# A conditioned decoder step: the two MLP products by blocks with seven half-size products each

## The chip, the core and the metric

The kernel runs on one core of a Trainium2 chip. Its engines work side by side and are tied by semaphores: TensorE (PE; its weight loads are shown as PEld), VectorE (DVE), ScalarE (ACT), GpSimd (POOL), and SyncE (SP), which here only issues DMAs. The metric is the device time of one execution in microseconds (us); lower is better.

## The reference

```python
mod = silu(c) @ w_ada + b_ada            # six vectors: sh1, sc1, g1, sh2, sc2, g2
h = rmsnorm(x, norm1_g) * (1 + sc1) + sh1
y = mixer(h, ...)                        # pooling, short convolution and Conformer heads; w_in before, w_out behind
x = x + g1 * y
h = rmsnorm(x, norm2_g) * (1 + sc2) + sh2
x = x + g2 * (square(relu(h @ w_ff1)) @ w_ff2)
out = rmsnorm(x, final_g)
```

There are 1024 prompt tokens, which share one c, and 8 sample tokens with a c each, so N = 1032 columns; the model is 1024 wide, the MLP 4096. All is float32.

## The kernel before

Activations lie transposed, features on the 128 partitions and tokens along the row: xT is 8 blocks of 128 x 1032. Every large product is made in three parts: both operands are split into a high part (float32r, a rounded copy) and a low part (the rest), and the product is high·high + high·low + low·high. `product` does this for one output block: for each block of the contraction and each of the three parts, three matmuls of TW = 344 columns.

Weights arrive by DMA in `wraw` (two slots), ACT copies them rounded to `whi` (`high`, L534), POOL subtracts to give `wlo` (`low`, L459).

The mixer ends with w_out in two parts, `p1` (contraction blocks 0 to 4) and `p2` (5 to 7), eight output blocks each; after each of them DVE adds gate times product to xT (`residual`, L951, L953, L955).

The second norm stands between `p2` and the MLP. ACT squares the rows of xT (L563), DVE adds them (`add_squares`, L963), PE sums over the partitions (`token_sums`, L1269), DVE and ACT make the factor 1/rms per token, PE spreads it (`spread`, L1298), then DVE and ACT write hhi and hlo (`h_pre` L817, `h_high` L570, `h_low` L824); POOL does the sample columns (`sample_h`, L475 to L479). `keep_clock` (L1279) gives PE matmuls of no use in between, some of 512, 258, 172 and 128 columns.

The MLP runs in groups of FG = 4 hidden blocks, in a loop that works ahead by one group. `up` makes four hidden blocks (8 x 9 matmuls each), `hidden` squares the rectified result (ACT L670, DVE L1110), and splits it (ACT L673, DVE L1114). `down` makes the share of these four blocks in all eight output blocks (4 x 9 matmuls each) and `residual` adds it to xT. Two sets of three PSUM banks alternate. The last group's `down` is done in three token tiles (`part`), so that the last norm and the output (`tile_sums`, `rows_out`) follow tile by tile.

Of the kernel before, what the change touches and what calls it, by code (L numbers as in the profile page):

```python
# [5 lines left out]
F32 = mybir.dt.float32  # L6
# [22 lines left out]
NG = FF_C // FG  # L29
# [3 lines left out]
ADA_SLOTS = 5  # L33
# [6 lines left out]
def plan():  # L40
# [42 lines left out]
    chunk("norm2", "-")  # L83
# [24 lines left out]
WARM = ((512,) * 5, (512,) * 2 + (258,) * 10 + (512,) * 2, (512,) * 4 + (172,) * 8 + (128,) * 8 + (512,) * 8)  # L108
LAG = 2
SQ = {2: 0, 3: CONV_C, 4: CONV_C + KD}  # L110
ADDED = {2: 0, 3: 1, 4: KD - 1}


def decoder_trunk(nc, x_prompt, x_sample, c_prompt, c_sample, state_pool, state_sconv, state_conf,
# [11 lines left out]
    with ctx:  # L126

        xT = sb("xT", [P, KD, N])
        whi = sb("whi", [P, 2, 8, P], F32R)
        wlo = sb("wlo", [P, 2, 8, P], F32R)  # L130
        wraw = sb("wraw", [P, 2, 8 * P])
        work = [sb(f"work{i}", [P, PAD + N]) for i in range(3)]
# [19 lines left out]
        last_cols = sb("last_cols", [P, 2, P])  # L152
        states_out = sb("states_out", [P, 2, P])
# [32 lines left out]
        hid_hi = sb("hid_hi", [P, 2 * FG, N], F32R)
        hid_lo = sb("hid_lo", [P, 2 * FG, N], F32R)

        acc = ctx.enter_context(nc.psum_tensor("acc", [P, 2, 3, 512], F32))
        modps = ctx.enter_context(nc.psum_tensor("modps", [P, 512], F32))  # L190
        tps = ctx.enter_context(nc.psum_tensor("tps", [P, 512], F32))
# [1417 lines left out]
```

## Time and profile before

| | |
|---|---|
| median of 3 runs (lowest to highest) | 1138.33 us (1138.1 to 1138.94) |
| the profiled execution | 1138.9 us, span 1136.8 us |
| mean granted clock of TensorE | 0.983 |
| PE, DVE, ACT, POOL busy | 97%, 47%, 22%, 22% |
| DMA | 83.15 MB, mean 73 GB/s |

The span runs from the first to the last instruction of the core; the rest of the execution's time lies around it. Busy time counts an engine's instructions with a waiting time for operands or ports in them; a busy PE is one whose matmuls follow each other.

### The profile page before, as it was taken

To read this page: it belongs to the slowest core of one execution; us is meant where nothing else is said; L and a number is where in the kernel's file an instruction comes from. 1 tells how busy PE (TensorE), PEld (TensorE's weight loads), DVE (VectorE), ACT (ScalarE), POOL (GpSimd) and SP (SyncE) were. 2 spreads that over 40 slices of the span, in tenths; PEclk is the share of its full clock that TensorE was granted. 3 is DMA by queue.
4 is the path that set the end of the run, shared out by engine and by line. 5 is a ranking of instruction groups with operands and counts; after the bars stand their busy time and mean duration, and the time that the engine had idled before them with its cause. 6 is when DMAs were issued, how large, how long until landed. Compare 5 with 4: busy or idle time off the path is not lost.

```text
span 1136.8 us, 16478 instructions
## 1 busy us (share of the span) xinstructions
PE 1108.3 (97%) x7060; PEld 1078.0 (95%) x7060; DVE 531.0 (47%) x670; ACT 244.6 (22%) x269; POOL 255.5 (22%) x190
## 2 busy tenths in 40 slices
PE   7899999999999999999999999999999999999996
PEld 5688889999999899999999999999999999999996
DVE  4899999996367731222132223122222222312355
ACT  6321121112234332211210311220221130122111
POOL 2732122221112121212121212121212121213200
PEclk8899999999899899999999999999999999999999
DMA  9988211201111011111111111111111111111212
GB/s 282 319 294 304 66 38 38 56 24 47 29 56 56 19 48 46 55 39 54 40 52 42 44 50 43 51 41 54 38 56 38 55 39 55 39 55 41 72 51 99
DMA packets 97172, 83.15 MB, mean 73 GB/s; under 512 B 2663, under 2 KB 92718, under 8 KB 95039
## 3 DMA queue, kind: packets, MB, share of 16 engines
q1 hardware_dynamic: 96350, 80.87, 23.0%
q8 instruction: 59, 0.97, 0.3%
q0 software_dynamic: 336, 0.58, 0.2%
q10 hardware_dynamic: 417, 0.65, 0.2%
q14 instruction: 10, 0.08, 0.0%
HBM read 77.77 MB, written 4.81 MB: 73 GB/s over the span
## 4 chain that ended last, share of the span: by engine, by line
PE 88%; DVE 7%; SPq 2%; issue 1%; DMA 1%; POOL 0%; ACT 0%; DVEq 0%; POOLq 0%
PE acc L1237 76%; PE acc L1258 4%; DVE dc L895 4%; SPq L346 1%; PE acc L1528 1%; PE acc L1526 1%; PE acc L1527 1%; PE tps L1269 1%; DMA ada<-in_w_ada 1%; PE modps L1371 1%; DVE work L914 1%; PE acc L1555 1%; PE modps L1349 1%; DVE work L1178 1%; PE modps L1279 1%
## 5 line engine op out<-in xcount | busy, mean ns | idle before, releaser
L459 POOL TENSOR_TENSOR wlo<-wraw,whi 128x1024 fp32r<-128x1024 f32 (+2 forms) x89 | 210.2, 2362 | 785.3 <-ACT whi L534 785.3
L534 ACT ACTIVATE whi<-wraw 128x1024 fp32r<-128x1024 f32 (+2 forms) x89 | 90.9, 1022 | 684.4 <-PE acc L1237 644.7
L1237 PE MATMUL acc<-hhi,whi 128*128 128x344 f32 x1080 | 230.4, 322 | 2.1 <-issue 1.5
L1237 PE MATMUL acc<-hlo,whi 128*128 128x344 f32 x1080 | 229.0, 320 | 0.0
L1237 PE MATMUL acc<-hhi,wlo 128*128 128x344 f32 x1080 | 228.1, 320 | 0.0
L1237 PEld LDWEIGHTS acc<-hhi,whi 128*128 128x128 f32 x1080 | 181.4, 188 | 6.7 <-issue 6.5
L1237 PEld LDWEIGHTS acc<-hlo,whi 128*128 128x128 f32 x1080 | 182.6, 189 | 0.0
L1237 PEld LDWEIGHTS acc<-hhi,wlo 128*128 128x128 f32 x1080 | 180.1, 188 | 0.0
L951 DVE SCALAR_TENSOR_TENSOR xT<-acc,modT,xT 128x688 f32<-128x688 f32 x72 | 67.2, 934 | 236.7 <-PE acc L1237 235.9
L1110 DVE SCALAR_TENSOR_TENSOR work<-acc,work 128x1032 f32<-128x1032 f32 x32 | 39.4, 1232 | 249.7 <-ACT work L670 249.7
L1237 PE MATMUL acc<-hid_hi,whi 128*128 128x344 f32 x672 | 142.2, 320 | 0.0
L1237 PE MATMUL acc<-hid_lo,whi 128*128 128x344 f32 x672 | 142.0, 320 | 0.0
L1237 PE MATMUL acc<-hid_hi,wlo 128*128 128x344 f32 x672 | 142.0, 320 | 0.0
L895 DVE SCALAR_TENSOR_TENSOR dc<-glu,tapT,dc 128x1023 f32<-128x1023 f32 (+14 forms) x90 | 136.3, 1515 | 2.9
L1237 PEld LDWEIGHTS acc<-hid_lo,whi 128*128 128x128 f32 x672 | 113.0, 188 | 0.0
L1237 PEld LDWEIGHTS acc<-hid_hi,whi 128*128 128x128 f32 x672 | 112.6, 188 | 0.0
L1237 PEld LDWEIGHTS acc<-hid_hi,wlo 128*128 128x128 f32 x672 | 112.4, 188 | 0.0
L1114 DVE TENSOR_TENSOR hid_lo<-work,hid_hi 128x1032 fp32r<-128x1032 f32 x32 | 39.5, 1233 | 39.1 <-ACT hid_hi L673 39.1
L673 ACT ACTIVATE hid_hi<-work 128x1032 fp32r<-128x1032 f32 x32 | 34.1, 1067 | 42.1 <-DVE work L1110 42.1
L953 DVE SCALAR_TENSOR_TENSOR xT<-acc,modT,xT 128x336 f32<-128x336 f32 x72 | 40.2, 558 | 0.0
L670 ACT ACTIVATE work<-acc 128x1032 f32<-128x1032 f32 x32 | 32.5, 1015 | 0.0
L1526 PE MATMUL acc<-hid_hi,hhi 128*128 128x344 f32 x96 | 31.2, 325 | 0.0
(181 smaller groups left out, 981.3 us busy)
## 6 DMA issues: line engine op xcount, KB each, us to landing
wraw<-in_w_ff SPq DMA_DIRECT2D x64, 512.0 KB, 3.8
ada<-in_w_ada SPq DMA_DIRECT2D x16, 1024.0 KB, 8.4
wraw<-in_w_in SPq DMA_DIRECT2D x17, 512.0 KB, 4.7
ada<-in_w_ada SPq DMA_DIRECT2D x16, 512.0 KB, 7.4
xrow<-in_x_prompt SPq DMA_DIRECT2D x8, 512.0 KB, 9.0
out<-work SPq DMA_DIRECT2D x6, 512.0 KB
wraw<-in_w_out SPq DMA_DIRECT2D x8, 320.0 KB, 3.2
wraw<-in_w_out SPq DMA_DIRECT2D x4, 384.0 KB, 3.1
```

The source lines that it names most:

```text
L459: nc.gpsimd.tensor_tensor(o, a, b, ALU.subtract).then_inc(wlo_ready, 1)
L534: nc.scalar.activation(whi[:, slot, 0:n, :].rearrange("p k n -> p (k n)"), wraw[:, slot, 0:n * P], ACT.Copy).then_inc(whi_ready, 1)
L670: nc.scalar.activation(tiled(wk[0]), flat(acc[:, (C_FF + j) % 2, :, :]), ACT.Relu).then_inc(relu_ready, 1)
L673: nc.scalar.activation(hid_hi[:, slot + j, :], wk[1 + j % 2][:], ACT.Copy).then_inc(hid_hi_ready, 1)
L895: ins = nc.vector.scalar_tensor_tensor(dc[:, c, s:T], glu[:, c, 0:T - s], tapT[:, tap:tap + 1], dc[:, c, s:T], ALU.mult, ALU.add)
L951: nc.vector.scalar_tensor_tensor(pair(xT[:, d, 0:2 * TW]), ps[:, 0:2, 0:TW], g1, pair(xT[:, d, 0:2 * TW]), ALU.mult, ALU.add)
L953: nc.vector.scalar_tensor_tensor(xT[:, d, 2 * TW:T], ps[:, 2, 0:w2], g1, xT[:, d, 2 * TW:T], ALU.mult, ALU.add)
L1110: nc.vector.scalar_tensor_tensor(tiled(q), flat(acc[:, (C_FF + j) % 2, :, :]), 0.0, tiled(wk[0]), ALU.max, ALU.mult).then_inc(freed_v, 1)
L1114: nc.vector.tensor_tensor(hid_lo[:, slot + j, :], q[:], hid_hi[:, slot + j, :].bitcast(F32), ALU.subtract).then_inc(hid_lo_ready, 1)
L1237: last = nc.tensor.matmul(out[:, t, 0:TW], w[:, slot, b, :], x[:, k, t * TW:(t + 1) * TW], start=(i == 0 and w is whi and x is hi), stop=( ...
L1258: last = nc.tensor.matmul(outs[j][:, t, 0:TW], w[:, (u0 + j) % 2, k, :], x[:, k, t * TW:(t + 1) * TW], start=(k == 0 and w is whi and x is ...
L1526: nc.tensor.matmul(bank[:, 0:TW], w_hi, hi[:, k, cols], start=(b == 0), stop=False)
```

## The change

Both MLP products are made by blocks of 2 x 2 with seven half-size products in place of eight (Strassen's scheme in Winograd's form).

*Up.* A unit is 256 hidden features (two blocks m). The contraction is cut in pairs of blocks (KP = 4), the tokens in two halves of 524 columns (two tiles of HT = 262: 256 tokens, columns for the shift and for the samples). POOL makes the weight sums (`mix_weights`), ACT and POOL split the seven weights in four groups (`high_split`, `low_split`), each with one buffer; the operand sums are made once (`mix_rows`, `mix`, `oper_high`, `oper_low`). PE makes product p as 4 x 3 x 2 matmuls. Products share banks X, Y and V and go on accumulating in them: p0, p2, p4, p6 in X, p1 in Y, p3, p5 in V. After p0, p2 and p3 ACT copies the bank to a tile C (`copy_c`), DVE adds the bank after p1, p4 and p5 (`add_c`), and takes p6 as it is (`last_c`).

*Second norm.* The products are made from x times gain, without the factor of the token; the factor `rb` is multiplied in behind them (`scale_c`), the shift rides along as a column (`shift_c`). The sums for it are made during unit 1. norm2's stage and `keep_clock` are gone.

*Between.* `activate` (ACT) makes relu and square of each quarter C, DVE its four sums (`mix_hidden`), and SP stores seven tiles of 128 x 524 a unit in DRAM (`hid_home`; four tiles for the last two units, without sums). xT's storage is used for the tiles C, so x is stored in DRAM as well (`x_home`) and returns late (`return_x`, `rejoin`).

*Down.* Seven groups of four hidden blocks; a group has four pairs of output blocks (m = 0 to 27), product p of a pair is 2 x 3 x 2 matmuls of QT = 258 columns, and DVE gathers each bank into y (`gather`). Two weight units to a group. The activations return through twelve stages (`load_queue`) and are split again (`queue_high` on ACT, `queue_low` on DVE). The eighth group is plain, in four token quarters (`part`, 384 matmuls).

*Other.* Four slots for w_ada instead of five; the samples' row comes out as a ninth block; all loops are written out.

```diff
-ADA_SLOTS = 5
+ADA_SLOTS = 4
+HT = 262
+QT = 258
+NP = 7
+KP = 4
+UP = FF_C // 2
+GROUPS = 7
+PAIRS = 4
+FIRST_OF_CHAIN = (0, 1, 3)
+GROUP_ENDS = (1, 3, 5, 6)
...
+            def mix_weights(unit):
+                pool.wait_ge(raw_loaded[unit % 2], raw_at(unit))
+                if unit:
+                    pool.wait_ge(split_lo, 4 * unit)
...
+                link(nc.gpsimd.tensor_tensor(s3, a21, a11, ALU.subtract))
+                link(nc.gpsimd.tensor_tensor(a21, a21, a22, ALU.add))
+                link(nc.gpsimd.tensor_tensor(s2, a21, a11, ALU.subtract))
+                nc.gpsimd.tensor_tensor(s4, a12, s2, ALU.subtract).then_inc(mixed_ready, 1)
...
+            for unit in range(1, UP + 2 * GROUPS):
+                mix_weights(unit)
+                for g in range(4):
+                    low_split(unit, g)
...
+            def high_split(unit, g):
+                act.wait_ge(raw_loaded[unit % 2], raw_at(unit))
...
+                    act.wait_ge(product_made, spent(unit - 1, g))
+                if g:
+                    act.wait_ge(mixed_ready, unit + 1)
...
+            def activate(unit, n):
+                act.wait_ge(c_scaled, 4 * unit + n + 1)
+                tile = halves(c_tile(unit, n))
+                nc.scalar.activation(tile[:, :, 0:QT], tile[:, :, 0:QT], ACT.Relu, bias=tile[:, 0, 260:261]
+                                     ).then_inc(rect_ready, 1)
+                act.wait_ge(rect_ready, 4 * unit + n + 1)
+                nc.scalar.activation(tile[:, :, 0:QT], tile[:, :, 0:QT], ACT.Square).then_inc(hid_ready, 1)
...
+            for unit in range(2, UP):
+                copy_c(unit, 0, BANK_X[unit % 2], 0)
...
+                high_split(unit + 1, 0)
+                activate(unit, 0)
...
+                copy_c(unit, 2, BANK_X[unit % 2], 2)
...
+                copy_c(unit, 1, BANK_V, 3)
+                high_split(unit + 1, 1)
...
+                activate(unit, 1)
...
+                high_split(unit + 1, 2)
+                activate(unit, 2)
...
+                high_split(unit + 1, 3)
+                activate(unit, 3)
...
+            def mix_hidden(unit):
+                dve.wait_ge(hid_ready, 4 * unit + 4)
+                c11, c22, c21, c12 = [c_tile(unit, c) for c in range(4)]
+                nc.vector.tensor_tensor(c12, c12, c11, ALU.subtract).then_inc(t_ready, 1)
...
+                nc.vector.tensor_tensor(t_tile(2), c22, c12, ALU.subtract).then_inc(t_ready, 1)
+                dve.wait_ge(t_ready, 4 * unit + 2)
+                nc.vector.tensor_tensor(t_tile(3), c11, t_tile(2), ALU.subtract).then_inc(t_ready, 1)
+                nc.vector.tensor_tensor(t_tile(5), c21, t_tile(2), ALU.subtract).then_inc(t_ready, 1)
...
+            for unit in range(2, UP):
+                if unit < UP - 1:
+                    mix_hidden(unit - 1)
+                add_c(unit, 0, BANK_Y, 1, 1)
+                scale_c(unit, 0)
...
+                add_c(unit, 1, BANK_X[unit % 2], 4, 2)
+                scale_c(unit, 1)
...
+                add_c(unit, 2, BANK_V, 5, 3)
+                scale_c(unit, 2)
...
+                last_c(unit)
...
+                for j in range(PAIRS):
...
+                    gather(m + j, 0, g == 0)
+                    gather(m + j, 1, g == 0)
+                    if j < 3:
+                        queue_low(n + 3 * j)
+                    elif not last:
+                        queue_low(n + 8)
+                    gather(m + j, 2, g == 0)
...
+            def product_of(p, bank, blocks, tiles, pieces, width):
+                for n, i in enumerate(blocks):
+                    for w, x in ((0, 0), (0, 1), (1, 0)):
+                        for t in tiles:
+                            last = nc.tensor.matmul(banks[:, bank + t, 0:width], weight(p, w, i),
+                                                    operand(p, x, pieces[n], t, width),
...
+                product_of(0, x, every, both, every, HT).then_inc(product_made, 1)
...
+                product_of(1, BANK_Y, every, both, every, HT).then_inc(product_made, 1)
+                pe.wait_ge(copied, ahead + 1)
+                pe.wait_ge(split_lo, split_at(unit, 1))
+                product_of(2, x, every, both, every, HT).then_inc(product_made, 1)
...
+                product_of(3, BANK_V, every, both, every, HT).then_inc(product_made, 1)
...
+                pe.wait_ge(copied, ahead + 2)
+                pe.wait_ge(split_lo, split_at(unit, 2))
+                product_of(4, x, every, both, every, HT).then_inc(product_made, 1)
```

In the down loop (not shown) p2 of a pair waits for gather 0, p4 for gather 2, p5 for gather 3, p6 for gather 4; in the queue of DVE the fourth pair of a group has six queue_low, after gathers 1, 2, 4, 5 and twice after 6, the first two pairs three (after 1, 5, 6), the third two.

## Rows read from the trace of the kernel before

**Rows 1.** The page, part 1: busy us, share of the span, instructions.

```profile
PE 1108.3 (97%) x7060; PEld 1078.0 (95%) x7060; DVE 531.0 (47%) x670; ACT 244.6 (22%) x269; POOL 255.5 (22%) x190
```

**Rows 2.** The page, part 4: the chain that ended last, by engine.

```profile
PE 88%; DVE 7%; SPq 2%; issue 1%; DMA 1%; POOL 0%; ACT 0%; DVEq 0%; POOLq 0%
```

**Rows 3.** Windows by stage: length, busy of each engine (instructions), clock, DMA share, GB/s.

```profile
331.60:365.80 34.20, 34.13 (x217) 33.87 (x216) 21.77 (x33) 11.03 (x11) 7.95 (x4) 1.00 0.21 61
365.80:385.60 19.80, 18.28 (x87) 15.71 (x87) 11.90 (x19) 7.47 (x10) 7.55 (x6) 0.74 0.09 26
...
408.60:748.00 339.40, 338.66 (x2148) 338.38 (x2148) 88.14 (x115) 67.73 (x67) 72.17 (x30) 1.00 0.16 49
748.00:1066.00 318.00, 317.20 (x2013) 316.92 (x2012) 84.86 (x125) 58.60 (x57) 74.38 (x31) 1.00 0.17 50
1066.00:1136.80 70.80, 61.26 (x415) 59.42 (x413) 37.65 (x78) 11.98 (x27) 0.00 (x0) 0.97 0.16 61
```

**Rows 4.** PE, 172 columns: timeline (start, us to the last end), then group (mean ns).

```profile
381.03 1.04 PE L1279 MATMUL modps<-yc_hi 128*128 128x172 f32 x8
...
L1279 PE MATMUL modps<-yc_hi 128*128 128x172 f32 x8 | 1.0, 271 | 0.0
```

**Rows 5.** DVE's groups by shape: count, busy us, mean ns, idle before.

```profile
L951 DVE SCALAR_TENSOR_TENSOR xT<-acc,modT,xT 128x688 f32<-128x688 f32 x72 | 67.2, 934 | 236.7 <-PE acc L1237 235.9
L953 DVE SCALAR_TENSOR_TENSOR xT<-acc,modT,xT 128x336 f32<-128x336 f32 x72 | 40.2, 558 | 0.0
L1114 DVE TENSOR_TENSOR hid_lo<-work,hid_hi 128x1032 fp32r<-128x1032 f32 x32 | 39.5, 1233 | 39.1 <-ACT hid_hi L673 39.1
L1110 DVE SCALAR_TENSOR_TENSOR work<-acc,work 128x1032 f32<-128x1032 f32 x32 | 39.4, 1232 | 249.7 <-ACT work L670 249.7
...
L1161 DVE TENSOR_TENSOR work<-work 128x344 f32<-128x344 f32 x18 | 9.2, 514 | 7.2 <-ACT work L720 7.2
```

**Rows 6.** The same of POOL and of ACT.

```profile
L459 POOL TENSOR_TENSOR wlo<-wraw,whi 128x1024 fp32r<-128x1024 f32 x77 | 190.3, 2471 | 699.0 <-ACT whi L534 699.0
L459 POOL TENSOR_TENSOR wlo<-wraw,whi 128x640 fp32r<-128x640 f32 x8 | 12.5, 1564 | 62.1 <-ACT whi L534 62.1
...
L534 ACT ACTIVATE whi<-wraw 128x1024 fp32r<-128x1024 f32 x77 | 81.6, 1060 | 621.0 <-PE acc L1237 581.3 <-DMA wraw<-in_w_in 34.1 <-PE acc L1258 5.6
...
L554 ACT ACTIVATE work<-acc 128x344 f32<-128x344 f32 x6 | 2.7, 457 | 5.9 <-PE acc L1298 5.6
```

**Rows 7.** Two lines' durations (min/median/max ns), then timelines of DVE and POOL.

```profile
L967 DVE TENSOR_TENSOR small<-gate_s,modT x9: 224/2095/2133, 333.2 to 1070.5; 128x64 f32<-128x64 f32 x9
...
L1110 DVE SCALAR_TENSOR_TENSOR work<-acc,work x32: 1232/1232/1234, 406.5 to 1025.8; 128x1032 f32<-128x1032 f32 x32
...
358.44 2.40 POOL L459 TENSOR_TENSOR wlo<-wraw,whi 128x1024 fp32r<-128x1024 f32 x1 [6.90 <-ACT whi L534]
...
359.85 2.07 DVE L963 TENSOR_TENSOR work<-work 128x1024 f32<-128x1024 f32 x1 [1.13 <-ACT work L563]
...
366.97 2.37 POOL L459 TENSOR_TENSOR wlo<-wraw,whi 128x1024 fp32r<-128x1024 f32 x1 [6.13 <-ACT whi L534]
...
367.29 2.13 DVE L967 TENSOR_TENSOR small<-gate_s,modT 128x64 f32<-128x64 f32 x1
...
380.05 2.70 DVE L817 SCALAR_TENSOR_TENSOR work<-xT,A,work 128x1024 f32<-128x1024 f32 x2 [4.50 <-ACT work L554]
...
380.50 1.17 POOL L476 TENSOR_TENSOR hs<-hs,A 128x64 f32<-128x64 f32 x1
```

**Rows 8.** DMA issues of w_ada: count, KB each, median us to landing.

```profile
ada<-in_w_ada SPq DMA_DIRECT2D x16, 1024.0 KB, 8.4
```

**Rows 9.** PE in the norm: timeline, then windows with the granted clock.

```profile
366.70 1.03 PE L1269 MATMUL tps<-ones,work 128*128 128x1 f32 x8
...
368.00:370.00 2.00, 2.00 (x9) 0.51 0.00 0
370.00:378.00 8.00, 8.00 (x32) 0.50 0.23 66
```

More of the change, by code:

```diff
@@ new lines, in stage_loads, with queue_free, stored_tiles, stored_at @@
+def stage_loads(n):
+    return 16 * sum(stage_of(m) == stage_of(n) for m in range(n + 1))
+def queue_free(n):
+    g, p, _ = QUEUE[n]
+    if g == GROUPS:
+        return made(UP + PAIRS * (GROUPS - 2) + PAIRS - 1, 3 + p)
+    if g == 0 or (g == 1 and p >= 3):
+        return made(UP - 1, p)
+    return made(UP + PAIRS * (g - (2 if p >= 3 else 1)) + PAIRS - 1, p)
+def stored_tiles(unit):
+    return NP if unit < UP - 2 else 4
+def stored_at(unit):
+    return 16 * sum(stored_tiles(v) for v in range(unit % 2, unit + 1, 2))
@@ L186, in decoder_trunk @@
[L186 to L191, printed above, removed]
+        xrow = span(H_AT, KD * D).rearrange("p (i n) -> p i n", n=D)
+        rest = H_AT + KD * D
+        xsrow = span(rest, D)[0:S]
+        crow = span(rest + D, D)[0:32]
@@ new lines, in _, with queue_low @@
+            diagonals(3, diag2)
+            add_c(1, 0, BANK_Y, 1, 1)
+            dve.wait_ge(rb_ready, 3)
+            dve.wait_ge(copied, 4)
+            scale_c(0, 0)
+            scale_c(0, 1)
+            scale_c(0, 2)
+            scale_c(0, 3)
+            scale_c(1, 0)
+            add_c(1, 1, BANK_X[1], 4, 2)
+            scale_c(1, 1)
+            add_c(1, 2, BANK_V, 5, 3)
+            scale_c(1, 2)
+            mix_hidden(0)
+            last_c(1)
+            def queue_low(n):
+                dve.wait_ge(queue_hi, n + 1)
+                nc.vector.tensor_tensor(queue_piece(n, 1), stage(n), queue_piece(n, 0).bitcast(F32), ALU.subtract
+                                        ).then_inc(queue_lo, 1)
@@ L1532, in tile_sums, with operand @@
-            def tile_sums(t):
-                pe.wait_ge(ms_ready, 3 + t)
-                for d in (0, KD - 1):
-                    if d:
-                        pe.wait_ge(sq_ready, SQ[4] + t * KD + KD)
-                    else:
-                        pe.wait_ge(sq_added, ADDED[4] + (t + 1) * (KD - 2))
-                    for q in range(3):
-                        last = nc.tensor.matmul(tps[:, 3 * t + q:3 * t + q + 1], sq_part(d)[:, SUB[q]:SUB[q] + P],
-                                                ones[:, 0:1], start=(d == 0 and q == 0), stop=(d > 0),
-                                                skip_group_check=True)
+            def operand(p, h, i, t, width):
+                return halves(piece(i, h, p))[:, t, 0:width]
@@ new lines, in up @@
+            def up(p, bank, blocks, tiles):
+                for i in blocks:
+                    pe.wait_ge(oper_lo, LO_AT[i, p])
+                    last = product_of(p, bank, [i], tiles, [i], HT)
+                return last
+            every = range(KP)
+            both = (0, 1)
+            x0, x1 = BANK_X
+            freed(CHUNK_AT[("p2", KD - 2)])
+            pe.wait_ge(ext_ready, 1)
+            pe.wait_ge(split_lo, split_at(0, 0))
+            up(0, x0, (0, 1), (0,))
+            pe.wait_ge(split_lo, split_at(0, 1))
```

1416 lines of the change are left out of this document (1027 added, 389 removed).

## The prediction

> **What bounds the kernel now.** The first view is the busy time of each engine [rows 1]: TensorE (PE) is at 97%, VectorE (DVE) at 47%, GpSimd (POOL) and ScalarE (ACT) at 22%. The chain that ended last agrees: 88% of it is PE [rows 2]. The table by stage [rows 3] tells where the change strikes. The two MLP stages, 385.6 to 1066.0, are PE without a gap: 2148 matmuls in 339.4 us and 2013 in 318.0 us are 0.158 us for one of 344 columns. A hidden block pair (144 matmuls) costs 22.7 us and a group of four hidden blocks through the second matrix (288) 45.4 us. Ahead of them stand the second norm, 19.8 us at a clock of 0.74, and the last eight products of the mixer, 34.2 us. So fewer columns are worth their full price as long as PE stays the bound. What the reader should look at next is therefore who else works, and with whom.
>
> **Part 1, the matmuls.** An up unit (two hidden blocks) becomes 7 products of 24 matmuls of 262 columns, a down pair (two output blocks) 7 products of 12 of 258, four pairs to a group. No row has 258 columns at full clock. From below, 172 and 128 columns take (1.04-0.27)/7 = 0.11 us each [rows 4], the floor with a weight load for every matmul; from above, in proportion to the 0.158 of 344 columns, 0.120, and with that one's excess over 344/2.4 GHz kept whole, 0.124. I take 0.122 and 0.120. That is 2.93 us a product and 20.5 us a unit up (22.7 before), 1.44 us a product, 10.1 us a pair and 40.3 us a group down (45.4 before). The last group stays plain, 384 matmuls of 258 for 288 of 344, the same columns. PE alone would save 16 x 2.2 + 7 x 5.1 = 71 us.
> The Trainium skill (TensorE: Matmul & The Clock Gate, Back-to-back issue gap) gives an isolated gap of N/2.4 + 2.5 ns, 146 ns for 344 columns; this trace has 158. By the page a unit up would be estimated at 18.8 us and PE's saving larger; the row decides.
>
> **Part 2, what the vector engines get per up unit.** One element costs DVE 1.045 ns and an instruction 0.16 (344 and 1032 elements [rows 5]), so the 524-element ones take 0.70 us, from PSUM too. A unit has 3 add_c and last_c (PSUM), 3 scale_c, 4 mix_hidden (SBUF alone) and 4 small shift_c: 8.5 us. POOL takes 1.56 us for 640 elements and 2.47 for 1024 [rows 6], so 1.3 for 512: mix_weights 4 x 1.3, low_split 3 x 2.4 + 1.3, 13.7 us. ACT [rows 6]: splits of 1.06, copies of 0.6 (457 ns at 344), activate 1.45 for two passes: 11.5 us. All lie under 20.5 us, so the table of busy time would call them hidden. Two things are not in it.
> First, DVE and POOL exclude each other. L967, a DVE instruction of 64 elements, takes 0.22 us at best and 2.10 in the median of nine [rows 7]: at 367.29 it stood 2.13 us, until POOL's split of 366.97 ended. At 359.85 a sum of 1024 ended 1.08 us after POOL, as if it had begun 0.14 before POOL's end. In the other direction POOL's 64-element L476 takes 1.17 us beside DVE's L817, and gets in between two DVE instructions that need not wait for one another: they alternate. But L1110, with one operand in PSUM, takes 1.232 us in all 32 cases, always beside POOL. So scale_c, shift_c, mix_hidden, queue_low and the operand splits collide; add_c and gather do not.
> By the Trainium skill (SBUF — State Buffer, Who interferes with whom) a Vector instruction with two SBUF inputs blocks for the whole of a GpSimd instruction that reads SBUF; this trace agrees. It is the rule that speaks against this change.
> Second, order. p4 of unit u waits for copy_c(u,2); ahead of that in ACT's queue stands activate(u,0), which waits for scale_c(u,0), behind mix_hidden(u-1) in DVE's queue, which waits for activate(u-1,3), which waits for p6 of u-1. From p6's end: 0.3 to be seen, last_c 0.7, shift 0.25, activate 1.45, four mixes 2.9, add_c 0.75, scale 0.75, shift 0.25, activate 1.45, copy 0.65, 0.1: 9.55 us (10.15, since add_c also waits for p1). p4 could start after four products, 11.7. There are 1.55 us to spare without POOL. But POOL's low_split g3 is released by the same p6, and its four mixes and low_split g0 follow: 8.9 us of POOL in that very window. Alternating, and with 0.15 to 0.25 gained at each handover, the four mixes wait 0.85, 1.05, 1.05 and 1.05 and scale_c 1.4: p4 starts at 14.95, and with the three products after it the unit lasts 23.8 us. If low_split g2 beats the small shift_c of the unit before, it is 25.8. From below 20.5 (no wait), from above 27.3 (all 8.9 in full). I take 24.1, near the first, for the 12 units 3 to 14: 289 us. Unit 2 carries a backlog, 27.5; unit 15 has no mix_hidden, 21.5.
>
> **Part 3, down.** A pair gives DVE 7 gathers of 0.70 (PSUM, free of POOL) and 3.5 queue_low of 0.70, 7.4 us of 10.1. But PE may run only one product (1.44 us) ahead of its gathers, and POOL's splits, 2.4 us each, fall 4.3, 7.2 and 10.1 us into every second pair. Followed through by these durations, the queue_low after gather 6 of the second pair costs PE 1.3 us, and the fourth pair with six of them 0.95 + 3.5: 46.0 us a group, x 7 = 322 (before 45.4, 318). From below 40.3; from above, 14 waits of 2.2 less 11 us of slack, 60.
>
> **Part 4, mixer's end and second norm.** Removed: 19.8 us of norm2. Added on DVE from about 335 on: 28 splits and 16 mixes of 512 elements (0.67 each) 29.4, eight updates of 0.93 + 0.56 + 0.16 [rows 5] 13.3, some 29 small ones 6.5: 49 us; to it 2.5 of waiting for ACT and some 12 of the 22 us that POOL now works there. So the last operand comes at 398, not at 386, p6 ends at 402. In unit 1 PE's sums of squares wait for seven squares and five sums of 1.25, 6.5 us, and p6 waits for five scale_c that come in one burst, 8: it ends at 437 (before 385.6 + 2 x 22.7 = 431). From below, PE alone: 407.
>
> **Part 5, the rest.** Start of down: in unit 15 copy, activate and queue_high stand in one ACT queue and queue_low ahead of add_c; gather 0 comes at about 31 us of a unit whose p2 could go at 23.4: 8 us, and 3 for POOL and clock, 11 (0 to 15). The parked activations are 106 stores and 106 loads of 268 KB; 1 MB lands in 8.4 us in the crowded start [rows 8], so 7 tiles and 1 MB of weights need 24 at worst and about 14 by my reckoning, of 24 and 46 us: hidden, but x's return (4 MB) comes 3 late. Four ada slots for five: +1 (0 to 4). The tail, 70.8 us before, gets a ninth block of rows and shorter matmuls: 73.
>
> **Sum** on the span: 438 (437 + 1) + 27.5 + 289 + 21.5 + 11 + 322 + 3 + 73 = 1185. The span was 1136.8 in an execution of 1138.9, which is 0.6 above the median of 1138.33; so the time is 1185 + 1.5, 1186.5.
>
> **Rivals.** (a) PE stays the bound: POOL's work doesn't fall into the window, or costs under 1.55 us a unit there. Then units 2 to 15 take 14 x 20.5 = 287, down 282, the norm ends at 415: 415 + 287 + 5 + 282 + 75 = 1064. For it: no engine over 70% busy; against it: rows 7. Between it and the forecast lies a POOL that is blocked less than I reckon, break-even at 22.6 a unit with 43 a group. The forecast turns into a gain when two thirds of the port waits are missing. Chance of faster in all 0.30, of 1064 to 1085 0.12.
> (b) The forecast, port waits on the path: 0.52.
> (c) Worse: the idle of 3 to 4 us in each unit drops the clock. In the norm PE ran at 0.50, 1.2 GHz, from 368 to 378, after some 2 us in which it had only matmuls of one column [rows 9], and 10 us passed until it was back. A drop in every second unit costs 2 to 3 us each, with down at 50: 1215 to 1260. For it: rows 9; against: p0 to p3 are dense, four products in a row. 0.15.
> (d) The halves cancel, within 0.2%: 0.03.
> Less than 0.2% can't be told from no change here. Chances: faster 0.30, same 0.03, slower 0.67. The forecast's own range is 1150 to 1215; to leave out no more than 2 in 10 on both sides it has to reach into (a) and (c): 1090 to 1235.
>
> **What would show it.** Right: PE's stages up show an idle of 3 to 4 us ahead of p4 in each unit, released by ACT's copy; mix_hidden lasts 1.5 us and more instead of 0.70, and is longest where a POOL instruction ends with it; add_c stays at 0.70. Matmuls of 262 columns start 0.12 us apart. DVE's busy share rises over 70%. Wrong: PE over 97% busy between 440 and 1110, or mix_hidden at 0.70; then (a) holds. If one 262-column matmul takes 0.14, PE's part of the gain was never there.

## The result and the profile after

The changed kernel takes 1277.78 us (median of 4 runs, 1272.94 to 1284.38) against 1138.21 us: a ratio of 1.124, 95% interval 1.118 to 1.129. It is slower, as forecast, but by 140 us where 48 were expected, and outside the range of 1090 to 1235. The profiled execution has a span of 1281.8 us.

The page of the changed kernel, parts 1, 4 (the chain, by engine) and 5 (groups), beside [rows 1, 2, 5]:

```profile
PE 1098.7 (86%) x7811; PEld 1057.5 (83%) x7811; DVE 878.1 (69%) x1054; ACT 411.1 (32%) x584; POOL 564.8 (44%) x367
...
PE 48%; DVE 31%; issue 7%; ACT 6%; DMA 6%; SPq 1%; DVEq 0%; ACTq 0%
...
L2236 PE MATMUL banks<-split 128*128 128x262 f32 x2688 | 373.0, 305 | 79.3 <-ACT xT L1065 67.7
...
L2345 PE MATMUL banks<-split 128*128 128x258 f32 x2352 | 312.3, 296 | 61.6 <-DVE xT L1845 46.1
...
L1800 DVE TENSOR_TENSOR split<-plain,split 128x524 fp32r<-128x524 f32 x106 | 126.1, 1199 | 43.5 <-ACT split L1080 43.5
...
L1718 DVE TENSOR_TENSOR xT<-xT,banks 128x524 f32<-128x524 f32 x48 | 33.4, 696 | 131.2 <-PE banks L2236 131.2
...
L1730 DVE TENSOR_TENSOR xT<-xT 128x4 f32<-128x4 f32 x64 | 63.4, 990 | 2.2
```

PE had no idle worth the name before; now it has 79 us ahead of the up products, 68 of them ended by ACT's `copy_c` (L1065), and 62 ahead of the down products, most of them ended by DVE's `gather` (L1845). add_c (L1718, one operand in PSUM) takes 0.70 us, while queue_low (L1800), of the same size with both in SBUF, takes 1.20, and shift_c (L1730) takes 0.99 us for four elements.

Windows of the changed kernel by stage, beside [rows 3]. The stages are: end of the mixer; units 0 and 1 with the second norm; units 2 to 13; 14 and 15; the first 17 us of down; the rest of down; tail.

```profile
338.00:373.60 35.60, 28.07 (x175) 27.23 (x173) 32.16 (x40) 17.29 (x25) 14.93 (x8) 1.00 0.31 112
373.60:456.90 83.30, 57.92 (x384) 55.20 (x383) 52.96 (x79) 38.27 (x57) 39.28 (x20) 0.82 0.18 61
456.90:781.00 324.10, 275.00 (x2004) 272.29 (x2003) 185.41 (x182) 122.34 (x177) 185.28 (x96) 0.88 0.35 113
781.00:835.70 54.70, 44.62 (x331) 44.20 (x330) 28.94 (x34) 25.39 (x40) 27.06 (x16) 0.88 0.49 162
835.70:853.10 17.40, 6.58 (x44) 6.37 (x42) 10.42 (x12) 5.90 (x10) 9.49 (x6) 0.71 0.39 120
853.10:1209.30 356.20, 305.46 (x2313) 298.54 (x2312) 243.18 (x290) 107.50 (x147) 191.38 (x102) 0.93 0.36 121
1209.30:1281.80 72.50, 60.59 (x492) 59.21 (x491) 47.44 (x115) 14.92 (x37) 5.74 (x3) 0.94 0.17 66
```

The clock was 1.00 in both MLP stages before [rows 3] and is 0.88 and 0.93 now. Where it goes is seen in one unit, from the timeline of the changed kernel (start, duration, engine and line; the idle before and its releaser in brackets):

```profile
617.18 0.69 DVE L1739 TENSOR_TENSOR xT<-banks,misc 128x524 f32<-128x524 f32 x1
...
620.53 0.70 DVE L1748 TENSOR_TENSOR xT<-xT 128x524 f32<-128x524 f32 x1 [2.46 <-ACT xT L1075]
620.72 1.66 POOL L775 TENSOR_TENSOR plain<-plain 128x512 f32<-128x512 f32 x1
621.34 1.61 DVE L1752 TENSOR_TENSOR xT<-xT 128x524 f32<-128x524 f32 x1
...
624.17 1.64 POOL L777 TENSOR_TENSOR plain<-plain 128x512 f32<-128x512 f32 x1
624.58 1.79 DVE L1755 TENSOR_TENSOR xT<-xT 128x524 f32<-128x524 f32 x1
...
627.02 1.06 DVE L1725 TENSOR_TENSOR xT<-xT,misc 128x524 f32<-128x524 f32 x1
627.48 2.80 POOL L789 TENSOR_TENSOR split<-plain,split 128x1024 fp32r<-128x1024 f32 x1
628.12 2.18 DVE L1730 TENSOR_TENSOR xT<-xT 128x4 f32<-128x4 f32 x1
630.33 0.72 ACT L1072 ACTIVATE xT<-xT 128x516 f32<-128x516 f32 x1 [6.89 <-DVE xT L1730]
...
631.63 1.08 ACT L1065 ACTIVATE xT<-banks 128x524 f32<-128x524 f32 x2
...
632.27 1.02 PE L2236 MATMUL banks<-split 128*128 128x262 f32 x3 [4.15 <-ACT xT L1065]
```

This is the forecast chain, name by name: last_c, activate, four mixes (L1748 to L1755) that alternate with POOL's, add_c, scale_c, shift_c, activate, copy_c, p4. PE stood 4.15 us ahead of p4, mix_hidden took up to 1.79 us and add_c stayed at 0.70, as the prediction had said it would look; only DVE's share, 69%, stayed just under the 70% named there. What the sum did not have comes next. Windows of the unit before, by clock:

```profile
600.00:603.70 3.70, 0.81 (x7) 0.60 (x5) 2.96 (x2) 0.67 (x1) 2.98 (x2) 0.98 0.74 281
603.70:605.00 1.30, 0.03 (x1) 0.03 (x1) 0.00 (x0) 1.27 (x4) 0.00 (x0) 0.50 0.00 0
605.00:610.40 5.40, 5.40 (x25) 5.40 (x26) 0.00 (x0) 1.36 (x2) 2.37 (x1) 0.50 0.00 0
```

During the stop the clock falls to its lower level, 1.2 GHz; p4 starts in it and works 5.4 us at half speed (25 matmuls where the full clock does 44). The same happened in every unit from 3 to 14: they follow each other 27.3 us apart (the starts of last_c from unit 3 to unit 14: 508.2 to 808.3, 11 x 27.28).

In the down stage a group of four pairs takes 51.2 us (groups 2 to 6). Its timeline where PE stops:

```profile
1001.60 1.92 SPq L602 DMA_DIRECT2D plain<-in_w_ff  x4
...
1003.62 5.10 SPq L641 DMA_DIRECT2D plain<-hid_home  x8
...
1008.74 5.40 ACT L1080 ACTIVATE split<-plain 128x524 fp32r<-128x524 f32 x8 [9.15 <-DMA plain<-hid_home]
1009.41 0.70 DVE L1800 TENSOR_TENSOR split<-plain,split 128x524 fp32r<-128x524 f32 x1 [4.20 <-ACT split L1080]
1010.03 1.28 DVE L1845 TENSOR_TENSOR xT<-xT,banks 128x516 f32<-128x516 f32 x2
1010.77 7.51 PE L2345 MATMUL banks<-split 128*128 128x258 f32 x39 [3.16 <-DVE xT L1845]
```

SP issues the parked tiles (L641) behind 1 MB of weights (L602) that had to wait for POOL. The first lands at 1008.7. PE doesn't need it in this group, but queue_low, which does, stands ahead of gather 2 in DVE's queue, and p4 needs that gather's bank. It is the second stop of the group: 6 us earlier PE had already stood 2.73 us, for a gather behind queue_low and POOL's low_split. Behind the second stop too PE worked at half clock (0.57 from 1010.7 to 1017.5).

### The profile page after: what moved, and what is told of

Same layout as the page of the kernel before. It is cut to its first block, busy times and chain, and to the rows that moved or that the text cites. A ratio compares the mean times of both kernels' runs of the same rounds, so it can differ in the third digit from the quotient of the medians.

```text
span 1281.8 us, 19113 instructions
## 1 busy us (share of the span) xinstructions
PE 1098.7 (86%) x7811; PEld 1057.5 (83%) x7811; DVE 878.1 (69%) x1054; ACT 411.1 (32%) x584; POOL 564.8 (44%) x367
## 4 chain that ended last, share of the span: by engine, by line
PE 48%; DVE 31%; issue 7%; ACT 6%; DMA 6%; SPq 1%; DVEq 0%; ACTq 0%
PE banks L2345 16%; PE banks L2008 15%; PE banks L2236 10%; DVE split L1800 5%; DVE xT L1730 4%; PE banks L2395 3%; DMA plain<-hid_home 3%; DVE plain L1383 3%; DVE xT L1725 2%; ACT xT L1072 2%; DVE xT L1755 2%; DVE xT L1752 2%; DVE xT L1718 2%; DVE xT L1845 2%; DVE split L1597 1%
## 5 line engine op out<-in xcount | busy, mean ns | idle before, releaser
L2236 PE MATMUL banks<-split 128*128 128x262 f32 x2688 | 373.0, 305 | 79.3 <-ACT xT L1065 67.7
L2236 PEld LDWEIGHTS banks<-split 128*128 128x128 f32 x2688 | 367.3, 210 | 85.0 <-ACT xT L1065 71.3
L789 POOL TENSOR_TENSOR split<-plain,split 128x1024 fp32r<-128x1024 f32 (+1 forms) x120 | 275.1, 2298 | 357.3 <-ACT split L1012 357.3
L2345 PE MATMUL banks<-split 128*128 128x258 f32 x2352 | 312.3, 296 | 61.6 <-DVE xT L1845 46.1
L2345 PEld LDWEIGHTS banks<-split 128*128 128x128 f32 x2352 | 305.0, 202 | 68.7 <-DVE xT L1845 52.0
L2008 PEld LDWEIGHTS banks<-split 128*128 128x128 f32 x1656 | 262.8, 189 | 13.9 <-issue 8.5
L2008 PE MATMUL banks<-split 128*128 128x344 f32 x1656 | 266.9, 322 | 8.1 <-DVE gate_s L1443 7.5
L1845 DVE TENSOR_TENSOR xT<-xT,banks 128x516 f32<-128x516 f32 x180 | 123.4, 689 | 82.0 <-PE banks L2345 75.5
L1800 DVE TENSOR_TENSOR split<-plain,split 128x524 fp32r<-128x524 f32 x106 | 126.1, 1199 | 43.5 <-ACT split L1080 43.5
L1012 ACT ACTIVATE split<-plain 128x1024 fp32r<-128x1024 f32 (+1 forms) x120 | 113.7, 949 | 114.8 <-PE banks L2345 70.3
L1383 DVE SCALAR_TENSOR_TENSOR plain<-plain 128x1023 f32<-128x1023 f32 (+14 forms) x90 | 136.4, 1516 | 2.9
L1718 DVE TENSOR_TENSOR xT<-xT,banks 128x524 f32<-128x524 f32 x48 | 33.4, 696 | 131.2 <-PE banks L2236 131.2
L845 ACT ACTIVATE split<-plain 128x1024 fp32r<-128x1024 f32 (+2 forms) x29 | 27.3, 942 | 199.5 <-PE banks L2008 166.4
L1730 DVE TENSOR_TENSOR xT<-xT 128x4 f32<-128x4 f32 x64 | 63.4, 990 | 2.2
L2395 PE MATMUL banks<-split 128*128 128x258 f32 x384 | 50.3, 290 | 4.1 <-DVE gate_s L1903 4.1
L775 POOL TENSOR_TENSOR plain<-plain 128x512 f32<-128x512 f32 x30 | 45.7, 1524 | 16.7 <-DMA plain<-in_w_ff 12.6
L2395 PEld LDWEIGHTS banks<-split 128*128 128x128 f32 x384 | 48.3, 195 | 4.3 <-DVE gate_s L1903 4.3
L776 POOL TENSOR_TENSOR plain<-plain 128x512 f32<-128x512 f32 x30 | 46.4, 1548 | 2.4
```

Source lines behind the costliest of these rows:

```text
L789: nc.gpsimd.tensor_tensor(split_of(g, 1), split_source(unit, g), split_of(g, 0).bitcast(F32), ALU.subtract).then_inc(split_lo, 1)
L1012: nc.scalar.activation(split_of(g, 0), src, ACT.Copy).then_inc(split_hi, 1)
L1383: ins = nc.vector.scalar_tensor_tensor(dc[:, c, s:T], glu[:, c, 0:T - s], tapT[:, tap:tap + 1], dc[:, c, s:T], ALU.mult, ALU.add)
L1730: nc.vector.tensor_tensor(tile[:, :, 256:QT], tile[:, 1, 258:HT].rearrange("p (t s) -> p t s", t=2), tile[:, 0, 256:260].rearrange("p (t s ...
L1800: nc.vector.tensor_tensor(queue_piece(n, 1), stage(n), queue_piece(n, 0).bitcast(F32), ALU.subtract).then_inc(queue_lo, 1)
L1845: nc.vector.tensor_tensor(out, out, ps, ALU.add).then_inc(y_added, 1)
```

## The experiments

Behind each time stands its ratio to the kernel before on the same chip (1136.5 to 1138.5 us), with the 95% interval. A unit is read from the starts of last_c, a group from those of its last gather. A port wait is VectorE's wait for a running GpSimd instruction, as in Part 2 of the prediction.

**Port.** *e1_pool_small* shortens GpSimd's work from unit 1 on. The kernel then leaves out 7/8 of the weight sums and of the weights' low parts, which stay stale:

```diff
+                if unit:
+                    a11, a12, a21, a22, s3, s2, s4 = [a[..., 0:16] for a in (a11, a12, a21, a22, s3, s2, s4)]
...
-                nc.gpsimd.tensor_tensor(split_of(g, 1), split_source(unit, g), split_of(g, 0).bitcast(F32),
-                                        ALU.subtract).then_inc(split_lo, 1)
+                n = 16 if unit else P
+                nc.gpsimd.tensor_tensor(split_of(g, 1)[..., 0:n], split_source(unit, g)[..., 0:n],
+                                        split_of(g, 0).bitcast(F32)[..., 0:n], ALU.subtract).then_inc(split_lo, 1)
```

> GpSimd's mix_weights and low_split treat 16 of each 128 columns from unit 1 on; the other low parts of the weights stay stale. Its instructions shrink from 1.6 and 2.3 us to about 0.3. Theory (port waits make p4 late, the idle drops the clock): mix_hidden falls to 0.7 us, units 3 to 14 go from 27.3 us to 20.5 to 21.0 at full clock; that is 6.5 x 13 = 85 us. A down group keeps its late tiles, 51.2 to 48 or 49, 7 x 2.5 = 18 us: about 1175 us. Rival, the order of the queues alone does it: less than 10 us gained. Rival, the clock falls from the load of the array itself and not from the idle: half clock still for 6.8 us in each unit, unit 24, about 1220.

Measured: 1152.45 us, 1.013 [1.009, 1.016]. Every unit from 3 to 14 takes 20.48 us, no stop, clock 1.00; the timeline has all four mixes at 0.70:

```profile
615.85 0.70 DVE L1751 TENSOR_TENSOR xT<-xT 128x524 f32<-128x524 f32 x1 [1.46 <-ACT xT L1078]
...
616.66 0.70 DVE L1755 TENSOR_TENSOR xT<-xT 128x524 f32<-128x524 f32 x1
```

So with GpSimd's instructions short nothing of the up stage's loss is left, clock included, and the order of the queues costs nothing there by itself. This run also gives TensorE its low parts sooner; e10, in which GpSimd does all its work, rules that out as the reason. Groups 45.1 to 47.7: more than expected came back, the late tiles stayed.

**Order in ScalarE's queue.** *e2_copy_first* is shown (unit 15 keeps its order); *e8_both_copies* puts activate further down, behind copy_c(unit, 1):

```diff
                 high_split(unit + 1, 0)
-                activate(unit, 0)
                 if unit == UP - 1:
+                    activate(unit, 0)
...
                 copy_c(unit, 2, BANK_X[unit % 2], 2)
+                if unit < UP - 1:
+                    activate(unit, 0)
```

> Only the order in ScalarE's queue changes, units 2 to 14: copy_c(unit, 2) stands ahead of activate(unit, 0). Theory: GpSimd still blocks mix_hidden (1.6 us each), but p4 no longer hangs at the end of that chain: copy_c(unit, 2) comes with the end of p2, no idle ahead of p4, the clock stays full, unit 20.5 to 21.5 us, 13 x 6.4 = 83 us: about 1193 us; down unchanged at 51.2 a group. Rival, VectorE has no time left with its port waits: the wait moves to p6 (which waits for add_c(unit, 1)) or to p1 of the next unit, the clock still falls, unit 24 to 27: 1235 to 1275 us.

Measured: 1216.96 us, 1.069 [1.064, 1.074]. The clock stays at 1.00, but a unit takes 22.0, not 20.5 to 21.5. Its timeline:

```profile
617.65 0.61 ACT L1065 ACTIVATE xT<-banks 128x524 f32<-128x524 f32 x1 [1.79 <-PE banks L2238]
...
624.09 0.59 ACT L1065 ACTIVATE xT<-banks 128x524 f32<-128x524 f32 x1
...
624.73 1.48 PE L2238 MATMUL banks<-split 128*128 128x262 f32 x10 [1.26 <-ACT xT L1065]
```

copy_c(unit, 2) comes at 617.65 with p2's end; now the second copy, at 624.09, stands behind activate, and p5 waits for it. Neither theory had named that place.

> As the run with copy_c(unit, 2) first, but copy_c(unit, 1) too stands ahead of activate(unit, 0), units 2 to 14. There TensorE still stood 1.4 us ahead of p5 in each unit, which waits for copy_c(unit, 1). Theory: unit 22.0 to 20.5, 12 x 1.5 = 18 us less than that run's 1217: 1199. Rival, the wait moves on to p6 or p1: 22.0 and 1217.

Measured: 1196.41 us, 1.053 [1.049, 1.057]; a unit 20.82. As expected. Three of the four mixes still take 1.6 to 1.8 us: the port waits are there and cost PE 0.3 us a unit. So the stop took both, port waits and an order that hung the copies on them: e8 takes away the order, e1 and e10 the long waits.

**The clock by itself.** *e3_fillers*:

```diff
+                if 2 < unit < UP - 1:
+                    pe.wait_ge(c_added, added_at(unit - 1, 4))
+                    for _ in range(14):
+                        nc.tensor.matmul(banks[:, BANK_X[(unit + 1) % 2], :], piece(0, 0, 3)[:, 0:P],
+                                         piece(0, 0, 3)[:, 0:512], start=True, stop=True, skip_group_check=True)
                 pe.wait_ge(copied, ahead + 2)
```

> In units 3 to 14 TensorE does 14 more matmuls of 512 columns (3.0 us at full clock) between p3 and the wait ahead of p4, into a bank that is free; results unused. Theory (the idle drops the clock, half clock for 6.83 us costs 3.4 us a unit): idle under 0.5 us, full clock, unit 27.3 to 23.9, 12 x 3.4 = 41 us: about 1237 us. Rival, the clock falls whatever TensorE does: each unit still has 6.8 us at half clock and the time is 1278 or more. Rival, the drop is there but costs nothing since VectorE's chain sets the unit: unit stays 27.3, 1278.

Measured: 1251.95 us, 1.098 [1.094, 1.103]; a unit 24.97. Windows of eleven units of e3, then of ten of the changed kernel:

```profile
505.50:780.10 274.60, 263.87 (x2004) 253.37 (x2003) 171.74 (x166) 113.87 (x165) 171.38 (x89) 1.00 0.37 118
```

```profile
508.20:781.00 272.80, 231.26 (x1682) 229.19 (x1682) 155.58 (x152) 103.45 (x150) 154.97 (x81) 0.87 0.34 108
```

Fourteen more matmuls a unit, and the kernel is 26 us faster, where 41 were expected: the fall of the clock costs 2.3 us a unit, less than the 3.4 expected, because part of the slow time passes while PE stands. What is left, 25.0, is the wait with the clock kept; behind the added matmuls PE still stood 1.0 us.

**The place of the tiles.** *e4_tiles_first*:

```diff
+                for n in range(first, first + 6):
+                    load_queue(n)
                 load_raw(unit + 2)
-                for n in range(first, first + 8):
+                for n in range(first + 6, first + 8):
                     load_queue(n)
```

> Only SyncE's order changes in the down stage: six of the next group's parked tiles are loaded ahead of the next weights instead of behind them. Theory: the 2.5 to 3 us in which ScalarE waits for the tile and TensorE for the gather behind queue_low go, and with them the fall of the clock: a group goes from 51.2 to 46.5 to 47.5 us, 7 x 4.3 = 30 us: about 1248 us. Rival, queue_low behind GpSimd at the end of the group leaves TensorE idle long enough to drop the clock all the same: group 48 to 50, 1257 to 1270 us. Rival, the tiles are late because of the DMA rate, not of their place: no change.

Measured: 1254.51 us, 1.102 [1.100, 1.104], 6 us above the expected time. Groups 46.7 and 45.4 in turn; only every second one still loses its clock, and is 1.35 us longer for it. The stop that remains is the one of the forecast, queue_low behind low_split (timeline of e4):

```profile
985.25 4.62 POOL L791 TENSOR_TENSOR split<-plain,split 128x1024 fp32r<-128x1024 f32 x2 [1.11 <-ACT split L1014]
...
986.44 3.99 DVE L1802 TENSOR_TENSOR split<-plain,split 128x524 fp32r<-128x524 f32 x2
...
990.36 1.47 DVE L1847 TENSOR_TENSOR xT<-xT,banks 128x516 f32<-128x516 f32 x2
991.09 3.25 PE L2347 MATMUL banks<-split 128*128 128x258 f32 x18 [2.75 <-DVE xT L1847]
```

**The edges.** *e5_ends*, whose first part is

```diff
             square_row(5)
-            high_split(1, 0)
             copy_c(0, 2, BANK_X[0], 2)
             copy_c(0, 1, BANK_V, 3)
             square_row(6)
             square_row(7)
+            high_split(1, 0)
```

It answers to these rows of the changed kernel's timeline, where ACT's split of unit 1's weights waits for their DMA and two ready copies stand behind it:

```profile
398.97 1.01 SPq L595 DMA_DIRECT2D plain<-in_w_ff  x2
404.46 1.06 ACT L1012 ACTIVATE split<-plain 128x1024 fp32r<-128x1024 f32 x1 [5.21 <-DMA plain<-in_w_ff]
...
405.42 1.08 ACT L1065 ACTIVATE xT<-banks 128x524 f32<-128x524 f32 x2
...
406.06 1.24 PE L2236 MATMUL banks<-split 128*128 128x262 f32 x4 [8.54 <-ACT xT L1065]
```

> Two changes of order at the edges, the middle of both stages as in the changed kernel. (1) ScalarE's high_split(1, 0), which waits for weights whose load starts behind the last operand, goes behind copy_c(0, 2), copy_c(0, 1) and two squares: p4 of unit 0 starts at 400 instead of 406.1 and everything behind it 5 to 6 us earlier. (2) VectorE does add_c(15, 1) ahead of queue_low(4) to (7), last_c ahead of queue_low(10) and (11), and gather 0 to 3 ahead of queue_low(12) and (13): the 11.1 us of idle behind the second down product shrink to 2 to 4 us. Together 13 us: about 1264 us. Rival, the idle comes back behind the next wait (row sums behind GpSimd's splits; ScalarE's own queue in unit 15): 1272 to 1278.

Measured: 1265.87 us, 1.112 [1.110, 1.114], as expected in all. p4 of unit 0 started at 399.9; the idle behind the second down product came back in part behind the next wait (stops of 3.0 and 7.7 us).

**All orders together** (those of e8, in unit 15 too, of e4 and e5, the norm's row sums ahead of add_c on VectorE, and these), then the same with GpSimd small as in e1:

```diff
+                pe.wait_ge(c_added, added_at(unit - 1, 1))
+                product_of(1, BANK_Y, every, both, every, HT).then_inc(product_made, 1)
                 if unit == 1:
                     hidden_sums()
-                pe.wait_ge(c_added, added_at(unit - 1, 1))
-                product_of(1, BANK_Y, every, both, every, HT).then_inc(product_made, 1)
...
+            for n in range(LAST_Q, LAST_Q + 4):
+                load_queue(n)
             load_late(UP + 2 * GROUPS)
-            for n in range(LAST_Q, len(QUEUE)):
+            for d in range(4):
+                return_x(d)
+            for n in range(LAST_Q + 4, len(QUEUE)):
                 load_queue(n)
-            for d in range(6):
+            for d in range(4, 6):
                 return_x(d)
```

> The edges of the run before, both copies ahead of activate(unit, 0) in ScalarE's queue (units 2 to 15), tiles ahead of weights in SyncE's queue, the token sums of unit 1 behind its second product, x's return ahead of the last four tiles. Theory: up units 20.5 to 20.8 us with the clock full (27.3 before: -85), unit 15 23 (-10), start of down -8, groups 45.5 to 46.5 (-30), start -8, last group -5: 1278 - 146 = 1132, between 1120 and 1145. Rival, VectorE with its port waits stays the bound somewhere (unit 22 or more): 1150 and up, slower than the kernel before in either case.

Measured: 1157.86 us, 1.016 [1.014, 1.018]. The up stage did what was expected (20.83), but the groups take 45.4 to 47.9 and the first two units 8 us more than in the next run: still 1.6% slower than the kernel before, above the range expected.

> The run before with GpSimd's mix_weights and low_split on 16 of each 128 columns from unit 1 on (the other low parts stay stale). What is left is TensorE's floor and the edges: units 20.48, groups 40.3 to 41 us, 1075 us (1065 to 1090). Rival, the groups stay at 44 or more because queue_low and the gathers themselves hold TensorE: 1100.

Measured: 1098.13 us, 0.967 [0.964, 0.970]. Its span, 1095.4, is 65 us below e6's (60 in the medians), and nothing but GpSimd's instructions differs: that is what its work still cost there, port waits and waits for its results together, 46 us of it in the down stage (339.6 against 293.3). The kernel again leaves out most low parts. The estimate of 1075 was too low: unit 1 ends at 441.5 and the first group, with the start of down, takes 50. Windows of eleven units and of five groups of e7:

```profile
483.20:708.50 225.30, 225.30 (x1850) 225.30 (x1849) 94.38 (x166) 117.47 (x166) 39.37 (x88) 1.00 0.45 144
778.80:981.30 202.50, 202.50 (x1682) 202.13 (x1682) 140.10 (x211) 76.50 (x110) 35.70 (x81) 1.00 0.42 141
```

225.3 / 1850 and 202.5 / 1682 are 0.122 and 0.120 us a matmul.

**The same work in pieces.** *e10_quarters* keeps the changed kernel's orders, *e9_orders_quarters* has those of e6 (and the two row sums of the norm in pieces):

```diff
+            def short(out, a, b, op):
+                for k in range(0, out.shape[1], 2):
+                    ins = nc.gpsimd.tensor_tensor(out[:, k:k + 2], a[:, k:k + 2], b[:, k:k + 2], op)
+                return ins
...
-                link(nc.gpsimd.tensor_tensor(s3, a21, a11, ALU.subtract))
+                link(short(s3, a21, a11, ALU.subtract))
```

> The changed kernel with its own orders, and only GpSimd's mix_weights and low_split cut in pieces of 256 elements. Theory: mix_hidden 1.0 to 1.2 us instead of 1.6 to 1.8, scale_c 1.2 at most instead of 1.1 to 2.2, so p4 comes 2 to 3 us earlier, the idle ahead of it falls to 1 to 2 us and the clock stays up: unit 27.3 to 22 to 23.5 (12 x 4.5 = 54), groups 51.2 to 48 to 49 (late tiles stay): about 1208 us. Rival as in the other run of this pair: port waits the same, unit 27.3, 1278 or more.

Measured: 1189.95 us, 1.047 [1.044, 1.050]. A unit takes 20.48: better than the 22 to 23.5 expected, with the order untouched. Eleven units of e10:

```profile
490.00:715.30 225.30, 225.30 (x1850) 225.30 (x1850) 122.95 (x166) 117.04 (x166) 199.42 (x243) 1.00 0.46 144
```

Groups stay at 51, where 48 to 49 was expected. PE now comes to the late tile sooner and stands there once, 7.7 us, where it stood 2.7 and 3.1 us before (timeline of e10):

```profile
806.18 1.92 SPq L602 DMA_DIRECT2D plain<-in_w_ff  x4
...
815.63 2.73 PE L2350 MATMUL banks<-split 128*128 128x258 f32 x11 [7.65 <-DVE xT L1850]
```

> All orders as in the run of that name (1158), and GpSimd's instructions cut in pieces of 256 elements: same work, same results, four instructions for one of 1024, two for one of 512. Theory: what VectorE pays at a collision is the rest of GpSimd's running instruction, at most 0.7 us instead of 2.4; queue_low falls from 1.7 to 2.3 us to 1.0 to 1.3, groups from 46.7 to 47.8 us to 42 to 43 (TensorE's floor measured 40.5), 6 x 4.5 = 27; units 20.83 to 20.5 (-4), start -5: 1158 - 36 = 1122, between 1110 and 1130, faster than the kernel before (1138.5). Rival, a piece blocks as long as the whole instruction, since GpSimd's next piece takes the port again before VectorE gets it: 1155 to 1165, or slower for the added instructions (0.3 us each on GpSimd).

Measured: 1123.62 us, 0.989 [0.987, 0.991], 1.1% faster than the kernel before. Groups 41.2, units 20.48. queue_low between 500 and 1000 us, in e6 and then in e9:

```profile
L1797 DVE TENSOR_TENSOR split<-plain,split 128x524 fp32r<-128x524 f32 x85 | 105.0, 1246 | 10.8 <-ACT split L1086 10.7
```

```profile
L1805 DVE TENSOR_TENSOR split<-plain,split 128x524 fp32r<-128x524 f32 x98 | 91.9, 948 | 12.1 <-ACT split L1094 12.0
```

**What the trace of that run still showed:**

```diff
             for unit in range(1, UP + 2 * GROUPS):
+                if unit == 1:
+                    low_split(1, 0)
                 mix_weights(unit)
-                for g in range(4):
+                for g in range(unit == 1, 4):
...
             scale_c(0, 2)
+            add_c(1, 1, BANK_X[1], 4, 2)
             scale_c(0, 3)
             scale_c(1, 0)
-            add_c(1, 1, BANK_X[1], 4, 2)
```

> The orders and quarters of the run before (1123.6), and the idle stretches that its trace still shows taken away one by one: GpSimd does low_split(1, 0) ahead of mix_weights(1) (p0 of unit 1 stood 6.6 us for it: -5); add_c(1, 1) ahead of two scale_c (-1.7); queue_low(10) to (14) behind the gathers of the first down pair (3.7 and 4.3 us of idle: -6); in the last group ScalarE splits the last weights ahead of the last four tiles (4.4: -4); the last two rejoins among the first parts of the tail, and its weight splits in quarters (4.4: -3). Theory: all were waits of TensorE, so their sum of about 20 comes back: 1104, between 1098 and 1112. Rival: TensorE meets the next wait of the same chains a few us later, half of it comes back: 1113 to 1120.

Measured: 1112.43 us, 0.977 [0.975, 0.979]. 11 of the 20 us came back, the rival's number: part of the time behind p0 of unit 1 was lost again in a stop of 5.1 us ahead of p2 of unit 2 (its copy_c waited for the tile to be stored; 2.0 us in e9), and the first down pair's in three smaller ones. This is the version to keep: 2.3% faster than the kernel before, with the whole change in it.

## Why the prediction was wrong

The forecast's terms and the span measured, with units and groups as above (p6 of unit 1 itself ended at 454.4, last_c started at 456.9; unit 2 is short by as much):

| | forecast | measured | off |
|---|---|---|---|
| end of unit 1 | 438 | 456.9 | +19 |
| unit 2 | 27.5 | 24.2 | -3 |
| units 3 to 14 | 12 x 24.1 | 12 x 27.27 | +38 |
| unit 15 | 21.5 | 27.3 | +6 |
| start of down, first group | 11 + 46 | 61.4 | +4 |
| groups 2 to 6 | 5 x 46 | 5 x 51.2 | +26 |
| last group, x's return | 46 + 3 | 56.5 | +7 |
| tail | 73 | 72.5 | -0.5 |
| span | 1185 | 1281.8 | +97 |

**Part 1, right.** 0.122 and 0.120 us a matmul, as measured in e7; 20.48 us a unit and 40.5 a group without stops.

**Part 2, mechanism right, a term left out.** DVE and POOL alternate as said, in the named chain. e1 and e10 shortened its waits, e8 took TensorE's copies out of it, and the unit came back to 20.5 and 20.8; e2 moved one of the two copies and got 22.0. p4 came 16.0 us behind the start of its unit (27.3 less the 11.3 of p4 to p6, of which 5.4 us pass at half clock), not 14.95: last_c stood behind a shift_c that POOL held for 2.2 us, the case that the text priced at 25.8 and did not take. e3 shows 25.0 with the clock kept, 0.9 above the 24.1 taken. The other 2.3 us of each unit are the clock, 28 of the 38 us that units 3 to 14 are off. That a unit came to 27.3, the bound that Part 2 gives for a POOL in the way in full, is chance: it is 25.0 of waiting and 2.3 of clock. **This is the failed step:** the forecast has an idle of 3 to 4 us in each unit and counts full clock behind it. Rival (c) had the mechanism and its price, 2 to 3 us, but in every second unit with a chance of 0.15; it came in every one. The argument against it, that p0 to p3 are dense, speaks of the wrong side: what came before the stop did not prevent the fall. By the Trainium skill (TensorE: Matmul & The Clock Gate, HAM oscillation — how this bites in real kernels) throttled time times the missing share of the clock is the cost, by which the 6.7 us of the windows above would be an estimate of 3.4 us. This case has less: 1.3 of them found PE standing, p4 to p6 took 11.3 us, where e10 with the clock kept has 8.8, and e3 got 2.3 of these 2.5 back. Unit 15 (+6) is not part of this step alone: there p4 stood 5.9 us, 3.2 in e1, 2.1 in e6 and not at all in e7, where short GpSimd instructions and new orders come together.

**Part 3, the second failed step.** "Hidden, but x's return comes 3 late" reckoned the tiles' transfer by its length and left out its place in SP's queue, behind a load that waits for POOL. With the tiles first (e4) groups fell to 46.7 and 45.4, around the forecast's 46.0: its own price for the port was right. So 5 us in each of the groups 2 to 6, 25 in all, are the late tile and the clock behind it. The last group waits in the same way for four more tiles behind 1 MB, and then for x: with these moved (e6) it took 52.3 instead of 56.2 (e4). That is 4 of the +7; no run takes the rest apart.

**Part 4, off by 19.** The mixer's last products already waited for DVE (PE busy 28.1 of 35.6 us, before 34.1 of 34.2 [rows 3]), but the chain of operands hid it. The last operand came at 398.9, as forecast (398). Then p4 of unit 0 waited 8.5 us behind a split whose weights could not have been there (in e5 it started 6.2 us earlier), and p0 of unit 1 ended 5 us ahead of the row sums that POOL was holding up; the rows of that stretch show both:

```profile
409.80 11.31 POOL L789 TENSOR_TENSOR split<-plain,split 128x1024 fp32r<-128x1024 f32 x4
...
417.29 7.11 DVE L1763 TENSOR_TENSOR xT<-xT 128x1024 f32<-128x1024 f32 x3
...
424.54 0.77 PE L2039 MATMUL banks<-ones,xT 128*128 128x1 f32 x3 [5.22 <-DVE xT L1763]
```

Three sums of 1.25 us took 7.1. Both stops were followed by half clock. In e5 unit 1 ended 7 us earlier (449.8), in e7 15 (441.5), near the forecast. The edit that was costed by counting DVE's instructions was held by a DMA behind it and by POOL beside it.

**Part 5.** Tail right; ADA_SLOTS was not tried by itself; start of down 10.8 us of idle as the text had it, and 3.6 more behind it.

**Rivals.** (a) did not happen, but e7 shows its numbers for the stages (20.48 and 40.5). (b) gave the chain, (c) the rest. The range ended at 1235, inside (c)'s own 1215 to 1260; that case with a drop in all 16 units and its own 50 us for each of 7 groups, 1185 + 16 x 2.5 + 7 x 4 = 1253, was not worked out, nor was it joined with a late DMA.

The expected gain of PE's arithmetic is real in the two stages, then (20.48 us a unit and 40.5 a group in e7): it was lost to VectorE's waits for GpSimd and to tiles and weights that came late, and the longer of these stops were paid twice, as idle time and as clock.

## What to carry to other kernels

Where VectorE's two-operand work stands on the chain that feeds TensorE, give GpSimd its work in short instructions: it cost GpSimd about 0.15 us for each instruction more (199 us in eleven units against 177) and was worth 88 us here, more than any single reordering (81 in e8), though less than all orders together (120 in e6). When a forecast contains a stop of TensorE of some microseconds in a loop, price the clock behind each one, in every turn. And in each in-order queue (ScalarE's, SyncE's) ask what stands ahead of the instruction that others wait for: a copy behind an activation, tiles behind weights and a split behind a late load made three of the large stops, and a few moved lines undid each.

## What the runs showed of the hardware

- Stops of 1.0 us (e3) and 1.3 us (e2) in each of the units 3 to 14 never lowered the clock; stops of 4.2 us did, in each of them; of e4's stops of about 2.8 us, one to a group, every second one did (groups 2 to 6).
- A VectorE instruction of 4 elements takes 0.16 us alone and up to 2.24 beside a GpSimd instruction of 1024. The Trainium skill (SBUF — State Buffer, Who interferes with whom) says that a VectorE instruction with two SBUF inputs contends with a GpSimd instruction that reads SBUF, for ports that are an exclusive lock; the trace agrees. That the wait goes with the length of a single GpSimd instruction is what e9 and e10 show: in pieces of 256 elements mix_hidden took 1.05 to 1.24 us against 1.6 to 1.8, and queue_low 0.95 against 1.25.
- GpSimd's piece of 256 elements takes 0.73 us undisturbed, one of 1024 takes 2.4: four pieces 2.9.
